# Cross attention of a decoder trunk: the sample's chain placed half a chunk later under the V projection, K's turns in two parts, two more sample values behind V, and K copied out of PSUM by ScalarE

## What is computed

```python
def mem_kv(mem, norm_g, w_kv):          # prompt: K and V from 256 memory tokens
    k, v = jnp.split(rmsnorm(mem, norm_g) @ w_kv, 2, axis=-1)
    return (k.reshape(bsz, MEM_LEN, X_HEADS, X_HEAD_DIM), v.reshape(...))

def cross_attn(h, k, v, w_q, w_o):      # 4 heads of 256
    q = (h @ w_q).reshape(bsz, l, X_HEADS, X_HEAD_DIM)
    s = jnp.einsum('blhd,bmhd->bhlm', q, k) * (X_HEAD_DIM ** -0.5)
    p = jax.nn.softmax(s, axis=-1)
    o = jnp.einsum('bhlm,bmhd->blhd', p, v).reshape(bsz, l, D_MODEL)
    return o @ w_o
```

## Time and profile before

| | before |
|---|---|
| median of 3 runs | 1972.62 us (1968.41 to 1974.75) |
| the profiled execution | 1971.08 us, its span 1969.3 us |
| TensorE busy | 1807.1 us, 92% of the span |
| weight loads busy | 1652.3 us, 84% |
| VectorE busy | 1305.8 us, 66% |
| ScalarE busy | 867.0 us, 44% |
| GpSimd busy | 211.8 us, 11% |
| chain that ended last | TensorE 67%, VectorE 12%, ScalarE 11%, issue 6%, DMA 3% |
| mean granted TensorE clock | 0.968 of full |

### The profile page before, as it was taken

How to read it: one execution, slowest core, us unless ns; L and a number is a source line. 1 busy time by engine, 2 the same in 40 slices (tenths; PEclk the granted TensorE clock), 3 DMA queues, 4 the chain that set the end, 5 groups by cost and what they waited for, 6 DMA issues and landing times.

```text
span 1969.3 us, 34241 instructions
## 1 busy us (share of the span) xinstructions
PE 1807.1 (92%) x13440; PEld 1652.3 (84%) x13440; DVE 1305.8 (66%) x2287; ACT 867.0 (44%) x1137; POOL 211.8 (11%) x305
## 2 busy tenths in 40 slices
PE   7999898888989889898899999999998798899998
PEld 7999898877865545887789999999986697789998
DVE  5765677796886665459667655765556768667654
ACT  5433455344657633343444334433444542444333
POOL 1001101100110011111120001000311021120001
PEclk9999999999999999899899999999999999999999
DMA  8656644434885678568446657665734568446653
GB/s 219 188 155 181 195 137 135 143 113 120 272 284 162 203 251 270 172 213 295 163 127 184 174 165 198 180 183 161 228 111 136 183 216 297 159 126 184 174 162 117
DMA packets 463584, 361.01 MB, mean 183 GB/s; under 512 B 14633, under 2 KB 435781, under 8 KB 463429
## 3 DMA queue, kind: packets, MB, share of 16 engines
q1 hardware_dynamic: 409904, 254.87, 44.1%
q0 software_dynamic: 20288, 71.94, 10.7%
q10 hardware_dynamic: 33280, 32.65, 4.9%
HBM read 320.95 MB, written 38.66 MB: 183 GB/s over the span
## 4 chain that ended last, share of the span: by engine, by line
PE 67%; DVE 12%; ACT 11%; issue 6%; DMA 3%; POOL 0%; ACTq 0%; DVEq 0%; SPq 0%; POOLq 0%
PE psum L259 18%; PE psum L260 18%; PE psum L261 18%; ACT whi L209 4%; DVE wlo L215 2%; PE psum L1704 2%; DMA raw<-in_w_xkv 2%; PE psum L819 1%; PE psum L473 1%; PE psum L584 1%; DVE eb L1340 1%; PE psum L2191 1%; PE psum L239 1%; DVE hb L1510 1%; PE psum L241 1%
## 5 line engine op out<-in xcount | busy, mean ns | idle before, releaser
L215 DVE TENSOR_TENSOR wlo<-raw,whi 128x2048 fp32r<-128x2048 f32 (+2 forms) x261 | 553.4, 2120 | 284.0 <-ACT whi L209 283.5
L259 PE MATMUL psum<-xnh,whi 128*128 128x264 f32 x2328 | 676.3, 290 | 7.4 <-DVE ht L1161 4.3
L260 PE MATMUL psum<-xnl,whi 128*128 128x264 f32 x2328 | 665.7, 286 | 0.0
L261 PE MATMUL psum<-xnh,wlo 128*128 128x264 f32 x2328 | 664.6, 286 | 0.0
L209 ACT ACTIVATE whi<-raw 128x2048 fp32r<-128x2048 f32 (+2 forms) x261 | 460.8, 1766 | 121.2 <-DMA raw<-in_w_ffn_out 55.3
L259 PEld LDWEIGHTS psum<-xnh,whi 128*128 128x128 f32 x2328 | 444.8, 191 | 27.2 <-issue 26.1
L260 PEld LDWEIGHTS psum<-xnl,whi 128*128 128x128 f32 x2328 | 445.0, 191 | 0.3
L261 PEld LDWEIGHTS psum<-xnh,wlo 128*128 128x128 f32 x2328 | 442.6, 190 | 0.0
L259 PE MATMUL psum<-Hh,whi 128*128 128x264 f32 x704 | 200.9, 285 | 0.0
L261 PE MATMUL psum<-Hh,wlo 128*128 128x264 f32 x704 | 200.0, 284 | 0.0
L260 PE MATMUL psum<-Hl,whi 128*128 128x264 f32 x704 | 199.1, 283 | 0.0
(11 more groups left out here) (559 smaller groups left out, 3074.0 us busy)
## 6 DMA issues: line engine op xcount, KB each, us to landing
raw<-in_w_ffn_in SPq DMA_DIRECT2D x176, 512.0 KB, 4.9
raw<-in_w_in_ab SPq DMA_DIRECT2D x88, 512.0 KB, 4.5
raw<-in_w_ffn_out SPq DMA_DIRECT2D x64, 384.0 KB, 4.0
raw<-in_w_ffn_out SPq DMA_DIRECT2D x64, 320.0 KB, 3.4
sb<-in_state_ret POOLq DMA_DIRECT2D x32, 512.0 KB, 4.8
out<-sb ACTq DMA_DIRECT2D x32, 512.0 KB, 4.0
raw<-in_w_out_ab SPq DMA_DIRECT2D x32, 512.0 KB, 5.4
kc<-in_cache_mem_k POOLq DMA_DIRECT2D x32, 512.0 KB, 6.4
```

What stands on the lines that cost most here:

```text
L215: nc.vector.tensor_tensor(wlo[:, c % SLOTS, 0:m], raw[:, c % SLOTS, 0:m], whi[:, c % SLOTS, 0:m].bitcast(F32), ALU.subtract).then_inc(lo_d ...
L259: e.matmul(out, a, hi[:, kk, 0:S.cols], start=first, stop=False)
L260: e.matmul(out, a, lo[:, kk, 0:S.cols], start=False, stop=False)
L261: m = e.matmul(out, b, hi[:, kk, 0:S.cols], start=False, stop=final)
```

## The change

K's projection hands its PSUM banks to ScalarE (new `copy_out_act`, which first waits for Q's last bank) in place of VectorE. `v_out` waits for K's last bank ahead of V's first. `k_turn` becomes two stages of two turns each, one before and one after `prob_turn`. Under V, `score_turn` moves from the end of chunk 0 to the middle of chunk 1, `SampleSoftmax` from the middle to the end of chunk 1, `prob_turn` from there to the middle of chunk 2, `MaskProbs` and `SP_[1]` from the middle to the end of chunk 2. `SV[0]` moves from the middle of chunk 2 to the middle of chunk 3, `SV[1]` to the end of chunk 3. `SV[2]` and `SV[3]` go behind V, between the prompt's values, so six of eight sample values stand there and not four. In the middle of chunk 3 the first turns of the prompt's probabilities come ahead of the sample value. Each SP_[b+2] now stands right behind SV[b].

```diff
@@ -429,6 +429,15 @@
                                 ALU.mult).then_inc(bank_free, 1)
             return dve
 
+        def copy_out_act(dst, n, first):
+
+
+            def act(e, l, par, use):
+                if isinstance(l, int) and l == 0:
+                    first(e)
+                nc.scalar.activation(dst[:, bass.ds(l * 2, 2), :], psum[:, 2 * par:2 * par + 2, 0:n], ACT.Copy).then_inc(bank_free, 1)
+            return act
+
         rstd_two = rstd1[:, :, :].to_broadcast([P, 2, T])
 
         def scaled_out(dst, scale=1.0):
@@ -2098,15 +2107,18 @@
             score_turn = behind(lambda: Turn([([(B.sc[:, m_, :], P, 32, m_ * P) for m_ in range(2)],
                 lambda e, bank, par: mv(e, par, B.ps_[:, :], bank[0:32, 0:MEM]))], ready=at_least(X["kused"], 2 * NS * (lc + 1))))
             s_ready = turned()
-            Linear(W, 4, KD, 2, by_cols(W, 0), (B.mh, B.ml), kwise=tot["app"] - KD, dve=copy_out(B.Kf, n=MEM), cols=MEM,
+            Linear(W, 4, KD, 2, by_cols(W, 0), (B.mh, B.ml), kwise=tot["app"] - KD, act=copy_out_act(B.Kf, MEM, q_out), cols=MEM,
                    mid={1: [units[1]], 2: [units[3]], 3: [units[5]]}, hooks={0: [q_rows, units[0]], 1: [units[2]], 2: [units[4]], 3: [FirstV(), units[6]]})
             k_out = evicted()
 
             def v_out(e, l, par, use):
+                if l == 0:
+                    k_out(e)
                 e.tensor_copy(B.Vt[:, :, bass.ds(l * 256, 256)], psum[:, 2 * par:2 * par + 2, 0:256]).then_inc(bank_free, 1)
-            k_turn = behind(lambda: Turn([([(B.Kf[:, k0 + q, b * P:(b + 1) * P], P, P, q * P) for q in range(4)],
-                lambda e, bank, par, b=b, k0=k0: mv(e, par, B.Kt[:, b, k0 * P:(k0 + 4) * P], bank)) for b in range(2) for k0 in (0, 4)], ready=k_out))
-            kt_ready = turned()
+            def k_turn(b):
+                return behind(lambda: Turn([([(B.Kf[:, k0 + q, b * P:(b + 1) * P], P, P, q * P) for q in range(4)],
+                    lambda e, bank, par, k0=k0: mv(e, par, B.Kt[:, b, k0 * P:(k0 + 4) * P], bank)) for k0 in (0, 4)], ready=k_out))
+            k_turns = [k_turn(0)]
             class SampleSoftmax(Stage):
                 def dve(S, e):
                     s_ready(e)
@@ -2123,6 +2135,8 @@
             prob_turn = behind(lambda: Turn([([(B.ps_[:, m_ * P:(m_ + 1) * P], 32, P, m_ * 32) for m_ in range(2)],
                 lambda e, bank, par: mv(e, par, B.pTs[:, :], bank[:, 0:64]))], ready=at_least(X["sprob"], lc + 1)))
             ps_ready = turned()
+            k_turns.append(k_turn(1))
+            kt_ready = turned()
             class MaskProbs(Stage):
 
 
@@ -2298,10 +2312,10 @@
 
             SV, SP_, SC = [SampleValues(b) for b in range(NS)], [SplitValues(b) for b in range(NS)], [Scores(h) for h in range(XH)]
             LV = Linear(W, 4, KD, 2, by_cols(W, D), (B.mh, B.ml), dve=v_out, cols=256, turned=True, early=True,
-                        mid={0: [units[7]], 1: [SampleSoftmax()] + k_turn + [SP_[0]], 2: [MaskProbs(), SP_[1], Divide(0), SV[0]],
-                             3: [SV[2], SP_[3], Divide(2)] + p_turns[0]},
-                        hooks={0: [SC[0]] + score_turn + [LaterV(), SC[1]], 1: prob_turn + [SC[2], SC[3]], 2: [SV[1], SP_[2]],
-                               3: [SV[3], SP_[4]] + p_turns[1]})
+                        mid={0: [units[7]], 1: score_turn + k_turns[0] + [SP_[0]], 2: prob_turn + k_turns[1] + [Divide(0)],
+                             3: p_turns[0] + [SV[0], SP_[2], Divide(2)]},
+                        hooks={0: [SC[0], LaterV(), SC[1]], 1: [SampleSoftmax(), SC[2], SC[3]], 2: [MaskProbs(), SP_[1]],
+                               3: p_turns[1] + [SV[1], SP_[3]]})
             kv_out = evicted()
 
             class Keep(Stage):
@@ -2315,7 +2329,7 @@
             tot["stores"] += 32
             pending.append((stored["pool"], tot["stores"]))
 
-            stages.extend([Values(0), SV[4], SP_[5], Values(1), SV[5], SP_[6], Values(2), SV[6], SP_[7], Values(3), SV[7], SampleRows(), SampleOut()])
+            stages.extend([Values(0), SV[2], SP_[4], Values(1), SV[3], SP_[5], Values(2), SV[4], SP_[6], Values(3), SV[5], SP_[7], SV[6], SV[7], SampleRows(), SampleOut()])
 
             Wo = A["w_xo"][layer]
             residual(Wo, 4, KD, 2, by_cols(Wo, 0), (B.oh, B.ol), 1.0, G_FFN2 + 8 * layer, ready=all_of(at_least(X["sol"], lc + 1), at_least(X["ol"], 8 * lc + 8)))
```

## The result

| | before | after |
|---|---|---|
| median | 1971.13 us (20 runs) | 1978.47 us (20 runs, 1964.53 to 1984.29) |
| ratio, 95% interval | | 1.0036 [1.0024, 1.0049] |
| the profiled execution | 1971.08 us, span 1969.3 | 1978.62 us, span 1976.7 |
| mean granted clock | 0.968 | 0.964 |

A forecast was written before the change was run, and what follows sets the result against it. The order of links in the engines' queues was taken to bound the kernel. Gains of 3.6 us, less 1.0 for loads and 2.3 for clock, left 0.3 us faster: 1972.3 us against median 1972.62, range 1966.0 to 1978.5.

The forecast's parts named there:

- K's turn: K's second turn under V: TensorE waits for VectorE's score copy, idle about 5 us in layer 0, 1.5 in layer 1.
- the p gap: Ahead of the last turns of p: a new TensorE wait of about 2.8 us, since Divide(2) stands behind a split.
- no wait for `pm`: Sign: TensorE's wait for the masked probabilities is gone in both layers.
- stores ahead of two loads: GpSimd's queue: stores of K and V issue at 975.4, ahead of the loads of samples 6 and 7.
- Three of the named signs: Among the signs: TensorE's longest V wait at K's turn; no vc wait above 2 us; last value's start 24 us behind it.
- The front: Up to the first value's end: 0.4 us later in layer 0, 0.9 in layer 1, before 0.3 gained for K.
- 0.3 for K: K leaving PSUM by ScalarE instead of VectorE: 0.3 us a layer gained, between 0 and 0.6.
- the back: First value's end to value 7's start: 29.9 us, against 32.6 in layer 0 and 31.5 in layer 1 today.
- one layer: Lower clock after the gap ahead of p's last turns: likeliest in one of two layers, 2.3 us.
- The loads: Samples 6 and 7 loading behind the stores: load 6 lands between 982 and 987, 0.5 us a layer taken.
- Rival D: Gaps bring the lower clock each time, ahead of p and between values 6 and 7: 1978.4 us, chance 0.14.
- C's mechanism: Rival: loads behind the stores delay values 6 and 7, 3 us a layer: 1977.3 us, chance 0.16.

The follow-up runs named there:

- e10: Repeat of e5 (kernel after, K and V stores behind the loads of samples 6 and 7, Divide(2) ahead of value 0's split): 1965.31 us, 0.9958.
- e5: Kernel after, with the K and V stores behind the loads of samples 6 and 7 and Divide(2) ahead of value 0's split: 1963.78 us, 0.9958.
- e6: Kernel after, with only Divide(2) put ahead of value 0's split in the middle of V's last chunk: 1968.51 us, 0.9981.
- e1: Kernel after, with only the stage that stores K and V moved behind the loads of samples 6 and 7 on GpSimd's queue: 1976.68 us, 1.0033.
- e4: Kernel after, with K copied out of PSUM by VectorE as before the change: 1980.45 us, 1.0046.
- e8: Kernel after, with 24 matmuls that nothing reads put into the wait ahead of p's last turns: 1977.18 us, 1.0017.
- e11: Kernel after, with only the sample scores' turn put back to the end of V's chunk 0: 1976.57 us, 1.0021.
- e7: e5 with the sample scores' turn put back to the end of V's chunk 0: 1967.11 us, 0.9981.
- e3: Kernel before, with only K copied out of PSUM by ScalarE, V's first bank waiting for K's last: 1972.64 us, 1.0004.
- e9: e7 with the samples' softmax put behind the fourth score stage instead of ahead of the third: 1958.51 us, 0.9921.
- e12: e9 measured once more, unchanged: 1960.42 us, 0.9939.

## Why the prediction was wrong

**Right in kind.** The new waits came where the working put them. K's turn is released by VectorE's copy, which stands behind a weight split; the p gap is 2.86 us in both layers (forecast 2.8), 5.66 us from the first value's end to p's last turns (5.6); no wait for `pm`; stores ahead of two loads. Three of the named signs spoke against it: TensorE's longest wait in V is not at K's turn but ahead of SC[1] (2.91 and 6.36 us), ScalarE waits 4.70 us for sample 6, and value 7 starts 28.5 us behind p's turns, not 24. VectorE in the kernel after:

```profile
938.07 2.29 DVE L215 TENSOR_TENSOR wlo<-raw,whi 128x2048 fp32r<-128x2048 f32 x1 [1.82 <-ACT whi L209]
940.28 0.40 DVE L613 COPY ps__151<-psum 32x256 f32<-32x256 f32 x1
```

**The front: 1.6 us longer, not 0.35.** The gap at K's turn was 2.3 us in both layers, not 5 and 1.5, and the clock fell in both, where I had let it stay in layer 1. TensorE arrived later than worked out, since SC[1] ran at the lower clock. And VectorE's split of V's fourth chunk, which I had tied to that chunk's transfer, hung on SC[1]: the transfer was there, and ScalarE's split stood behind the last exponential of SC[1], as in all stretches but layer 0 of before. ScalarE in the kernel after:

```profile
935.67 0.47 ACT L2259 ACTIVATE pp<-psum,st 128x256 f32<-128x256 f32 x1 [0.81 <-DVE st L2254]
936.13 1.90 ACT L209 ACTIVATE whi<-raw 128x2048 fp32r<-128x2048 f32 x1
```

The fall at K's turn cost little. e10 is the same order with the clock up at that place; windows of 1 us, kernel after and then e10:

```profile
942.00:943.00 1.00, 1.00 (x6) 0.50 0.00 0
```

```profile
943.00:944.00 1.00, 1.00 (x11) 1.00 0.00 0
```

From K's turn to the end of the first value it is 21.6 us with the fall (kernel after, e5, e6, and layer 0 of e1) and 20.9 without it (e4, e8, e10, and layer 1 of e1); forecast was 20.4. So the fall costs 0.6 to 0.7 us where layer 0's was worked out at 2.7: the scores set the pace here, by VectorE and ScalarE. With the clock up, TensorE waits 1.33 us ahead of the fourth score stage for the exponential, with the fall 0.44. Before, K's turn came 10.1 to 10.9 us after SC[1], and the rest took 17.2 to 20.5. Now it comes 9.2 to 9.5 us after it in all but one case, so about 1 us earlier, but what follows takes 20.9 to 21.6. The front's forecast of 0.35 longer (0.4 and 0.9, less 0.3 for K) became 1.6.

**The term that failed most: the back,** 36.2 us against 33.65 by the forecast (29.9 to value 7's start, 2.1 for it, 0.5 for the loads, half of 2.3 for the clock). Together with the front's 1.25 this is 3.8 us a layer, the distance between 0.3 us faster and 7.3 slower. Of the 2.5 us:

- The clock fell ahead of p in both layers, where I counted one. The size of a fall, 2.3 us, was nearly right: 2.2 us between e1 (35.1) and e10 with the wait at p put back (32.9, below; in e1 the clock also fell during value 7), 1.6 between the kernel after and e11, in which it did not fall there. So the wrong count is worth about 1.1 us a layer by the forecast's size, 0.8 by the smaller one. Over all traces the clock fell after this 2.86 us gap in 6 of 8 cases, and after the gap of 3.06 us ahead of the old order's first value in 4 of 6. I had read "one layer" out of three gaps, with no row that speaks for the new place.
- The loads cost 1.1, not 0.5 (e1). They landed behind both stores. DMA issues of the kernel after (KB, us from issue to landing), store of V and the two samples:

```profile
out<-Vt POOLq DMA_DIRECT2D x1, 1024.0 KB, 7.5
vc<-in_cache_mem_v POOLq DMA_DIRECT2D x2, 512.0 KB, 8.5
vc<-in_cache_mem_v POOLq DMA_DIRECT2D x2, 512.0 KB, 9.2
```

  The stores went out at 978.2, not 975.4 as I had worked out, and sample 6 landed near 989 where I had bounded it by 987. By these rows the store of K landed at 982.8, that of V at 986.4, and the load behind them near 988.5: one after the other. In the kernel before, where nothing stood ahead of it on this queue, a load took 4.2 to 5.8 us. The Trainium skill (DMA: Bandwidth & Descriptors, Queues, rings and completion order) says that descriptors of one ring are taken in order; the trace agrees, with these 8.5 and 9.2 us.
- The rest, about 0.9, is in the chain of links itself, and no single link explains it. e10 shows it clean, with no wait at p and a clock that stays up: 29.9, of which 2.65 us from the first value's end to p's last turns. With the 5.66 us of the kernel after in their place it would be 32.9, against the 32.0 of the working. In layer 1 of e10 the turns and value 1 take 2.90 us to the drained end and not 2.75, an attention stage with its value 3.86 and 3.84 and not 3.6, and each later split starts 0.1 us after the end of the value that frees its buffer. The wait that I had put between values 6 and 7 stands there with timely loads (e1, e5, e10), and in the kernel after ahead of value 6.

**Where the signs went.** The forecast had the removed wait for `pm` and a cheaper interleaving pay for the new gap. But `pm` was late because of the order in VectorE's queue, and the new order puts Divide(2), the next thing due, behind a split in that same queue: the wait moved and hardly shrank (3.07 to 2.86 us). With Divide(2) a place earlier the idea works, as e6 shows. Rival D was the nearest in sum (1978.4) and in what it said of the clock; its falls ahead of p came in both layers, and its falls between values 6 and 7 came ahead of value 6. That its sum lies so near is in part luck, since it has nothing of the longer front. C's mechanism was there as well, at about a third of its price.

**What stays open.** When a gap of this length brings the lower clock: the same 2.73 us gap ended at full clock twice (e7) and at the lower one twice (e11). At K's second turn it never fell after a gap of 1.1 to 1.5 us (seven times), and after 2.2 to 2.4 us it fell in the seven cases of the new order and in neither of e3's two. (The expectation of e7 has 5 of 6 for the new order; the traces of the kernel after, e1 and e4 show 3 of 6, each after 2.3 us.) The Trainium skill (TensorE: Matmul & The Clock Gate, HAM oscillation — how this bites in real kernels) has waits between groups of matmuls throttle the array again and again; the traces agree for most of the gaps above 2 us, not for all. e1's small gain in whole time against 1.07 us a layer in the trace may have a part in it: in both layers the clock fell during value 7, and from the last value to the output projection it took 5.5 us in place of 3.8. But this trace is of e1's slowest execution, 1988.7 us, and the median is 1976.68. e9's and e12's size beside e5 rests on 6 timed runs each.

## What to carry to other kernels

A hand-written order is one order for every engine's queue: for each stage that moves, ask what it now stands behind on each of the five. Here a step of 1.4 us behind a split of 2.2 us cost 4 us a layer, with the fall of the clock that followed. Price a gap of 2 to 3 us on TensorE with its length and the slower clock behind it, and both at every place where it repeats, unless a row shows the clock holding there. A change that loses may hold a good idea with one step in the wrong place: each new wait, named and removed by itself, led from 1.0036 to 0.992 and 0.994.

## What the runs showed of the hardware

A load on GpSimd's queue behind two stores of 1 MB landed 8.5 to 9.2 us after its issue in the kernel after, against 4.2 to 5.8 us in the kernel before with nothing ahead, though it reads and they write. And a fall of the clock has no fixed price: 0.6 us at K's second turn, where other engines set the pace, 1.6 to 2.2 us ahead of p's last turns. Between the 20 executions of the kernel after the mean granted clock went with the time, loosely: 0.972 in the fastest (1964.5 us), 0.961 in the slowest (1984.3), 0.961 to 0.967 in the five above 1982, on average about 1.4 us for 0.001.
